# Reading and writing the 256 token columns of the feed-forward matmuls in alternating runs

## What is computed

```
def conv_ffn(h, w_up, conv_w, conv_b, w_down):          # layers 1 and 2
    a, b = jnp.split(h @ w_up, 2, axis=-1)
    a_pad = jnp.pad(a, ((0, 0), (CONV_WIDTH - 1, 0), (0, 0)))
    a = sum(a_pad[:, j:j + T] * conv_w[j] for j in range(CONV_WIDTH)) + conv_b
    return (jax.nn.silu(a) * b) @ w_down
# layer 3
ffn = (silu(n2 @ w_gate) * (n2 @ w_up)) @ w_down
```

## Time and profile before

| | |
|---|---|
| three runs | 903.50, 903.67, 904.66 us |
| the profiled execution | 904.41 us, its span 902.7 us |
| TensorE (PE) busy | 893.2 us, 99% of the span |
| weight loads (PEld) | 866.0 us, beside PE |
| VectorE (DVE) | 647.7 us, 72% |
| ScalarE (ACT) | 492.0 us, 54% |
| granted TensorE clock | 0.998 of full speed, the mean over the span |

### The profile page before, as it was taken

One profiled execution on the slowest core, in us unless ns is written; L12 is line 12 of the kernel. 1 busy time (PEld: TensorE's weight loads), 2 busy tenths in 40 slices (PEclk: granted clock), 3 DMA queues, 4 the chain that ended last, 5 costly groups with the idle time before them and its releaser, 6 DMA issues.

```text
span 902.7 us, 18665 instructions
## 1 busy us (share of the span) xinstructions
PE 893.2 (99%) x7875; PEld 866.0 (96%) x7875; DVE 647.7 (72%) x1188; ACT 492.0 (54%) x841; POOL 44.0 (5%) x50
## 2 busy tenths in 40 slices
PE   8999999999999999999999999999999999999998
PEld 7999999999999998789999999999988999999998
DVE  6887657877767689775887767677678486565664
ACT  6663555564545566674665546447437455444451
POOL 1000001000000000000100001001132000000000
PEclk9999999999999999999999999999999999999999
DMA  9643343565454543722556554654162255555541
GB/s 348 251 175 115 136 158 137 221 238 190 159 220 183 202 158 124 277 94 94 200 188 242 207 203 164 222 199 153 38 232 94 82 208 219 194 187 202 201 158 47
DMA packets 25570, 160.68 MB, mean 178 GB/s; under 512 B 2960, under 2 KB 4880, under 8 KB 6800
## 3 DMA queue, kind: packets, MB, share of 16 engines
q1 hardware_dynamic: 24912, 158.45, 47.9%
q10 hardware_dynamic: 576, 1.05, 0.3%
HBM read 158.18 MB, written 1.05 MB: 176 GB/s over the span
## 4 chain that ended last, share of the span: by engine, by line
PE 92%; DVE 5%; DMA 1%; ACT 1%; issue 0%; SPq 0%
PE ps L395 90%; PE ps L411 1%; DVE wl L1246 1%; DMA raw<-in_w 1%; DVE arena L1677 1%; ACT arena L2308 0%; DVE col L1254 0%; DVE arena L1693 0%; DVE arena L1976 0%; SPq L2534 0%; DVE arena L1672 0%; DVE arena L1747 0%; ACT arena L2066 0%; DVE arena L1964 0%; DVE arena L1304 0%
## 5 line engine op out<-in xcount | busy, mean ns | idle before, releaser
L1246 DVE TENSOR_TENSOR wl<-raw,wh 128x1024 fp32r<-128x1024 f32 x282 | 331.5, 1224 | 124.3 <-ACT wh L2036 124.0
L395 PE MATMUL ps<-xh,wh 128*128 128x256 f32 (+1 forms) x1264 | 352.4, 279 | 2.8 <-DVE wl L1461 1.6
L395 PE MATMUL ps<-xl,wh 128*128 128x256 f32 (+1 forms) x1264 | 350.3, 277 | 0.0
L395 PE MATMUL ps<-xh,wl 128*128 128x256 f32 (+1 forms) x1264 | 350.2, 277 | 0.0
L2036 ACT CAST wh<-raw 128x1024 fp32r<-128x1024 f32 x282 | 278.9, 1047 | 120.2 <-PE ps L395 107.9
L395 PEld LDWEIGHTS ps<-xh,wh 128*128 128x128 f32 x1264 | 237.6, 188 | 5.5 <-issue 2.3
L395 PEld LDWEIGHTS ps<-xh,wl 128*128 128x128 f32 x1264 | 237.7, 188 | 0.0
L395 PEld LDWEIGHTS ps<-xl,wh 128*128 128x128 f32 x1264 | 237.7, 188 | 0.0
L395 PE MATMUL ps<-fh,wh 128*128 128x256 f32 x528 | 145.7, 276 | 0.0
L395 PE MATMUL ps<-fl,wh 128*128 128x256 f32 x528 | 145.7, 276 | 0.0
L395 PE MATMUL ps<-fh,wl 128*128 128x256 f32 x528 | 145.7, 276 | 0.0
(11 more groups left out here) (249 smaller groups left out, 1047.6 us busy)
## 6 DMA issues: line engine op xcount, KB each, us to landing
raw<-in_w SPq DMA_DIRECT2D x145, 1024.0 KB, 4.9
raw<-in_w ACTq DMA_DIRECT2D x4, 256.0 KB, 5.7
xt<-in_x SPq DMA_DIRECT2D x4, 256.0 KB, 6.7
arena<-in_mem SPq DMA_DIRECT2D x1, 1024.0 KB, 8.8
out<-xt SPq DMA_DIRECT2D x8, 128.0 KB, 1.9
arena<-in_sel SPq DMA_DIRECT2D x3, 256.0 KB, 6.1
small<-in_small SPq DMA_DIRECT2D x1, 623.0 KB, 5.8
memkv<-in_gmask SPq DMA_DIRECT2D x1, 512.0 KB, 9.4
```

What stands on the lines that cost most here:

```text
L395: return pe.matmul(out, lhsT, rhs, start=start, stop=stop, skip_group_check=True)
L1246: v.tensor_tensor(L[:, s], src[:, s], f32(H[:, s]), ALU.subtract).then_inc(*w_lo.up(2 * S[i] + a))
```

## The change

A view `halves(ap, run)` reorders the 256 columns of an operand without moving data. With run 16 the order is columns 0 to 15, then 128 to 143, then 16 to 31, then 144 to 159, and so on; with run 0 it is the plain order. The moving operands and the PSUM output of a matmul get the same order, so each result lands in the column where it landed before. The u units use runs of 16 in f0, 4 in f1 and 16 in f2; the d units use 16 in f0, 4 in f1 and the plain order in f2. Nothing else differs: not the number of instructions, the operands' buffers, the waits or the other engines' programs.

```diff
+        def halves(ap, run):
+
+            return ap.rearrange("p (h a b) -> p a h b", h=2, b=run) if run else ap
+
...
-        def unit_f(name, bank, a_h, a_l, ready, two=None):
+        def unit_f(name, bank, a_h, a_l, ready, two=None, run=0):
...
-                    last = mm3(P[:, j * 256:j * 256 + T], H[:, c, o], L[:, c, o], x_h, x_l, c == 0 and j == 0, c == 7)
+                    last = mm3(halves(P[:, j * 256:j * 256 + T], run), H[:, c, o], L[:, c, o], halves(x_h, run), halves(x_l, run),
+                               c == 0 and j == 0, c == 7)
...
-        def down(tag, p):
+        def down(tag, p, run=0):
...
-                        last = mm3(acc, H[:, j, cs], L[:, j, cs], fch(fh_, f), fch(fl_, f), f == 0 and o % 2 == 0, False)
+                        last = mm3(halves(acc, run), H[:, j, cs], L[:, j, cs], halves(fch(fh_, f), run), halves(fch(fl_, f), run), f == 0 and o % 2 == 0, False)
...
         def ffn(tag):
             x_in = entered(tag)
...
+            run = {"f0": 16, "f1": 4, "f2": 16}[tag]
+            run_d = 0 if tag == "f2" else run
+            unit_f(f"{tag}u0", bank_a(), XH, XL, x_in, None, run)
...
+                down(tag, p, run_d)
```

More of the change, by code:

```diff
@@ L596, in down @@
                     f = 20 + j
-                    last = mm3(acc, H[:, j, cs], L[:, j, cs], fch(fh_, f), fch(fl_, f), False, j == 1)
+                    last = mm3(halves(acc, run), H[:, j, cs], L[:, j, cs], halves(fch(fh_, f), run), halves(fch(fl_, f), run), False, j == 1)
                 if o % 2 == 1:
@@ L612, in ffn @@
             x_in = entered(tag)
-            unit_f(f"{tag}u0", bank_a(), XH, XL, x_in)
-            unit_f(f"{tag}u1", bank_a(), XH, XL, x_in)
+            run = {"f0": 16, "f1": 4, "f2": 16}[tag]
+            run_d = 0 if tag == "f2" else run
+            unit_f(f"{tag}u0", bank_a(), XH, XL, x_in, None, run)
+            unit_f(f"{tag}u1", bank_a(), XH, XL, x_in, None, run)
             sums(tag, bank_b())
-            unit_f(f"{tag}u2", bank_a(), XH, XL, x_in, tag)
+            unit_f(f"{tag}u2", bank_a(), XH, XL, x_in, tag, run)
             norm_spread(tag, bank_b(), rst_)
[L618 to L622, removed]
+            unit_f(f"{tag}u3", bank_a(), XH, XL, x_in, tag, run)
+            unit_f(f"{tag}u4", bank_a(), XH, XL, x_in, None, run)
+            down(tag, 0, run_d)
+            unit_f(f"{tag}u5", bank_a(), XH, XL, x_in, tag, run)
+            down(tag, 1, run_d)
             for p in range(2, 10):
-                unit_f(f"{tag}u{2 * p + 2}", bank_a(), XH, XL, x_in, tag if tag == "f1" and p == 5 else None)
-                unit_f(f"{tag}u{2 * p + 3}", bank_a(), XH, XL, x_in)
-                down(tag, p)
+                unit_f(f"{tag}u{2 * p + 2}", bank_a(), XH, XL, x_in, tag if tag == "f1" and p == 5 else None, run)
+                unit_f(f"{tag}u{2 * p + 3}", bank_a(), XH, XL, x_in, None, run)
+                down(tag, p, run_d)
                 if tag == "f1" and p == 4:
                     meta_sums()
-            down(tag, 10)
+            down(tag, 10, run_d)
         t.wait_ge(*g_at0.at(0))
```

## The result

The changed kernel takes 943.89 us, the median of four runs (942.46 to 944.69), against 903.73 for the kernel before: 1.0437 times as long, 95% interval 1.0425 to 1.0449. The forecast was 886. The profiled execution has a span of 943.0 us.

The account below looks back on a forecast made before the run. The prediction took the matmuls' pace on TensorE to bound the kernel. Reads gain 17.2 us plus 1.1 us on the copies, writes and breaks 0: 904.4 - 18.3 = 886.1 us, own range 884 to 892, 8 in 10 range 884 to 911.

Parts of the forecast that it names:

- What bounds the kernel: Feed-forward blocks: the pace of the matmuls, 113.2 ns each, is the pace of the kernel.
- The count of 4224: Matmuls given a new order: 3168 in u units and 1056 in d units; f2's 528 d matmuls keep theirs.
- The reads: Moving operands of the changed matmuls: the new order ends overtaking of the weight stream, 113.2 to 109 ns, 18.3 us off.
- the transposes' 109: Pace in ns of 256 columns in the transposes, nearest row without visible stall, taken for the new order.
- The distances: Operand places modulo 256 bytes in changed matmuls: bad distances step by 118 ns, bounding the loss at 4.8 ns.
- The breaks: Between runs, 15 breaks per matmul in runs of 16, 63 in runs of 4: taken to cost 0.
- The writes: PSUM output written in the same runs: no wait moves, taken to cost 0.
- the lock: Rival, u and d matmuls in new order: streams lock on the same place, 19.7 us slower, 924 us; chance 0.14.
- The two rivals that put 112 or 113 down to a pace of the weight load itself: Changed matmuls: stall only cut, 5.6 us off, 898.8 us, chance 0.18; or nothing changes, 904 us, chance 0.18.
- The breaks rival: Changed matmuls: each break takes one column's 0.44 ns, together 61 us slower, 966 us; chance 0.08.
- What is late next: Other engines and transfers at 109 ns: VectorE fills 77%, weights still come in time, gain passes to the end undiminished.

## Why the prediction was wrong

**What bounds the kernel** was right: the pace of the matmuls is the time, 39.9 of 40.2 us come from the starts alone, and no engine or transfer came late. The count of 4224 was right as well.

**The reads** are the step that failed, together with the breaks below. I took the 4 ns between the transposes' 109 and the plain 113 for a collision with the weight load, and priced the new order at a gain of 18.3 us. No such gain exists here: no fp32r series of 256 columns came below 113.3, not even with a load of 32 columns. Nor has the load a part in what the runs cost: with 32 stationary columns in place of 128 it is 120.0 in runs of 16, as before, and 128.9 against 126.8 in runs of 4. The new order costs 6.7 ns a matmul in runs of 16 and 13.4 in runs of 4, 38.9 us in all, because the moving fp32r stream pays for not running on. Neither row that I priced it by held: the 109 is a float32 pace (0.85 ns for each of 128 columns, as the 0.84 of the float32 series), and the 118 is no fixed price of a distance.

**The distances.** The argument rested on 113 at 192 bytes and 118 at 64 and 128. The copies moved to 192 stepped by 118 and dragged the blocks with them, and later in f1 the same copies stepped by 113. A series at 64 bytes stepped by 113.3. So the distance alone does not decide. It is not without effect either, as the series with shifted starts and shifted weights show. Several rows from one kernel, each with its own history, could not tell place and history apart.

**The breaks** were taken at 0 on the evidence of the earlier trace rows. That evidence was float32, and float32 pays nothing for runs, as the three series of 215.8 ns show; it did not carry over to fp32r, where they make up 38.9 of the 40.2 us.

**The writes**, taken at 0, are free: 904.68 us with the writes alone in runs. The Trainium skill ("PSUM — Partial Sum Buffer", Specifications) has it that a pattern that is not contiguous slows matmuls; writing 256 sums in runs of 32, 16 or 4 left the pace at 113.3. The section that the prediction calls milder (the Trainium skill, "Advanced Engine Details and Errata", PSUM Cachelines) has that same rule beside its sentence on two consecutive elements, so it supported the 0 less than the prediction has it.

**The rivals.** The likeliest mechanism to the slow side had been the lock (924), and it is refuted as the cost of the runs with the collision. The two rivals that put 112 or 113 down to a pace of the weight load itself fall too: with 32 stationary columns the load's record shrank and the pace stayed at 113.3. The breaks rival, given 0.08, came nearest: its 0.44 ns a break was right for runs of 16 (6.7 / 15 = 0.45) and twice too much for runs of 4 (13.4 / 63 = 0.21), so that 966 stood where 944 was measured. It had been tied to the PSUM lines, while the cost lies in the reads. Its test, f1 much worse than f0 and f2, is what the trace shows.

**What is late next** did not arise.

## What to carry to other kernels

Read the moving operand of an fp32r matmul in runs of 64 columns or more; its output may be written in runs of 64, 32, 16 or 4, which cost nothing here. A price taken from rows of another type or another history is a guess: 40 copies of the disputed instruction inside the kernel measure it in 5 us, if a plain series ahead of each shows what pace it starts from. And when matmuls pace a kernel, compare the pace of like stretches, since a stretch can sit in a slower pace for what ran just before it.

## What was not expected of the hardware

- Plain fp32r matmuls of 256 columns hold one of two paces, 113.3 or 117.8 ns, over a whole block with the same operands; the one that is held follows from what came before, and it was worth 15 us here. Oddly placed copies, copies in runs of 4 and, once, the tiny matmuls of a norm with a unit on the copies were followed by 113, moved copies in plain order by 118. What holds a stretch in either is open.
- A shift of 16 bytes in the start of either operand, moving or stationary, raised plain order at once from 113.3 to 118.9 or 120.0. Whether that is the two streams meeting or something else is open.
- f2's unchanged d units stood at 118 or at 113 after u units in runs of 16: the same two paces, for 1.0 us in all.
- Sixteen columns read sixteen times over, so that each run starts where the last one did, step by 122.2 ns, no better than a jump of 512 bytes (120.0).
- 512 columns take 233.3 ns in plain order, more than two matmuls of 256 in the good pace (226.7); with plain reads and sums written in runs of 16 they took 228.9, so here too plain reads have more than one pace.
